# Sample attention with two score buffers, the second half's selection laid between the first half's products; 1 KB page pieces; a store issued later

## The reference

```python
kc, vc = compress(gather(cmp pages) ++ new)        # windows of 32 tokens, stride 16 -> two small products with a GELU
p_cmp = softmax(q @ kc + bias);    o_cmp = p_cmp @ vc
imp   = sum over a head group of p_cmp @ overlap   # importance of each block of 64 tokens
sel   = the blocks kept: 16 of 17, some always kept
p_sel = softmax(q @ k_sel + bias, only kept blocks); o_sel = p_sel @ v_sel   # the "sel" pages
p_win = softmax(q @ k_win + bias);  o_win = p_win @ v_win                    # the last 512 tokens
out   = g0 * o_cmp + g1 * o_sel + g2 * o_win
```

## Time and profile before

| | us |
|---|---|
| median of 3 runs | 1866.27 (1863.54 to 1869.59) |
| the profiled execution | 1865.92 |
| its span, first to last instruction | 1863.8 |
| `mixer_inputs` | 249.7 |
| `compress_phase` | 76.5 |
| `sample_attention` | 58.4 |
| the rest | 1479.2 |

### The profile page before, as it was taken

How to read it: one execution, slowest core, us unless ns; L and a number is a source line. 1 busy time by engine, 2 the same in 40 slices (tenths; PEclk the granted TensorE clock), 3 DMA queues, 4 the chain that set the end, 5 groups by cost and what they waited for, 6 DMA issues and landing times. The chain is left out here.

```text
span 1863.8 us, 28616 instructions
## 1 busy us (share of the span) xinstructions
PE 1775.2 (95%) x12010; PEld 1625.7 (87%) x12010; DVE 938.5 (50%) x1876; ACT 544.7 (29%) x1098; POOL 249.8 (13%) x110
## 2 busy tenths in 40 slices
PE   8999989589999899999978999999999999999997
PEld 6889978357767769999848999999999999999996
DVE  6422130467787664341533455545545555554547
ACT  7421000168888622210432221111111111111221
POOL 0111200000000000000000023313313322322320
PEclk9999999779999999999989999999999999999998
DMA  5122657621102241110261111101101101101102
GB/s 197 38 72 58 211 140 198 194 92 58 57 24 72 92 155 60 35 57 29 108 248 46 46 51 69 57 12 68 57 12 68 61 8 68 69 2 67 57 17 94
DMA packets 98308, 145.60 MB, mean 78 GB/s; under 512 B 40637, under 2 KB 73597, under 8 KB 96541
## 3 DMA queue, kind: packets, MB, share of 16 engines
q1 hardware_dynamic: 94094, 140.62, 22.7%
q10 hardware_dynamic: 4088, 3.17, 0.6%
HBM read 132.69 MB, written 14.19 MB: 79 GB/s over the span
## 5 line engine op out<-in xcount | busy, mean ns | idle before, releaser
L1963 PE MATMUL ps<-ff_in_high,ff_weights_low 128*128 128x352 f32 x1032 | 335.0, 325 | 0.0
L1963 PE MATMUL ps<-ff_in_high,ff_weights_high 128*128 128x352 f32 x1032 | 332.6, 322 | 0.0
L1963 PE MATMUL ps<-ff_in_low,ff_weights_high 128*128 128x352 f32 x1032 | 330.5, 320 | 0.0
L1963 PEld LDWEIGHTS ps<-ff_in_high,ff_weights_high 128*128 128x128 f32 x1032 | 194.4, 188 | 0.2
L1963 PEld LDWEIGHTS ps<-ff_in_low,ff_weights_high 128*128 128x128 f32 x1032 | 194.0, 188 | 0.2
L1963 PEld LDWEIGHTS ps<-ff_in_high,ff_weights_low 128*128 128x128 f32 x1032 | 193.7, 188 | 0.0
L2195 DVE TENSOR_TENSOR x<-ps,x 128x352 f32<-128x352 f32 x216 | 113.3, 524 | 134.6 <-PE ps L1981 134.6
L1932 POOL TENSOR_TENSOR ff_weights_low<-ff_weights,ff_weights_high 128x1024 fp32r<-128x1024 f32 x44 | 105.7, 2402 | 418.1 <-ACT ff_weights_high L2077 418.1
L1981 PE MATMUL ps<-ff_act_high,ff_down_high 128*128 128x352 f32 (+1 forms) x496 | 158.4, 319 | 0.2
L1981 PE MATMUL ps<-ff_act_high,ff_down_low 128*128 128x352 f32 (+1 forms) x496 | 156.6, 316 | 0.0
L1981 PE MATMUL ps<-ff_act_low,ff_down_high 128*128 128x352 f32 (+1 forms) x496 | 156.6, 316 | 0.0
(11 more groups left out here) (360 smaller groups left out, 3723.4 us busy)
## 6 DMA issues: line engine op xcount, KB each, us to landing
ff_weights<-in_w_up SPq DMA_DIRECT2D x22, 512.0 KB, 4.0
ff_weights<-in_w_gate SPq DMA_DIRECT2D x22, 512.0 KB, 4.3
ff_down<-in_w_down SPq DMA_DIRECT2D x22, 512.0 KB, 3.5
top<-in_mem_kt SPq DMA_DIRECT2D x8, 1024.0 KB, 10.9
top<-in_mem_v SPq DMA_DIRECT2D x8, 1024.0 KB, 13.5
x<-in_xt SPq DMA_DIRECT2D x3, 1408.0 KB, 10.0
x<-in_pool_cmp SPq DMA_DIRECT2D x32, 128.0 KB, 3.1
big<-in_pool_cmp SPq DMA_DIRECT2D x32, 128.0 KB, 2.8
```

What stands on the lines that cost most here:

```text
L1963: last = nc.tensor.matmul(K.bank[3 * s + x][:, 0:b - a], wt[:, s, ws], h[:, k, a:b], start=k + n == 0, stop=k == KD - 1 and n == 2)
```

## The change

Five edits go together.

1. A page lands as it lies in memory, keys and values side by side, 1 KB in one piece; `score`, `multiply` and `hidden_rows` read it with other strides.
2. At the start SP issues the first weight before the gains, and ACT runs one tiny instruction that needs no DMA, which brings its function table in.
3. The store `out_fm` moves from the end of `mixer_inputs` to `compress_phase`, behind the windows of half 0 and ahead of the sel pages of half 0.
4. In `compress_phase` round 0 waits for the first weight alone, round 1 for the second; the position sums of keys and values are made and closed one after the other, the second after round 0.
5. In `sample_attention` there are two places for scores and statistics. PE's order becomes: scores 0, importance 0, scores 1, transposes 0, then one importance step of half 1 and a third of half 0's products, three times, then the sums over the memory's squares, transposes 1, products 1. DVE adds half 1's bias before it copies half 0's transposed probabilities. ACT and DVE are reordered to fit.

```diff
--- before.py
+++ after.py
@@ -156,17 +156,13 @@
-    slots = K.slots[half]
-    if name == "cmp":
-        slots = slots.rearrange("p v (g t) -> p v g t", g=HKV)
     with sp.Fori(first, first + count) as n:
         sp.load(regs, K.page_table[0:1, bass.ds(n * NPAGE + half * (NS // 2) * NPAGE, NPAGE)])
         pages = [sp.snap(r, min_val=0, max_val=K.n_pool - 1) for r in regs]
         for b, page in enumerate(pages):
             of = K.pools[name][bass.ds(page, 1)]
-            of = of.rearrange("a p v g t -> (a p) v g t" if name == "cmp" else "a p v t -> (a p) v t")
-            to = slots[:, :, :, bass.ds(n * (NPAGE * PAGE // 2) + b * (PAGE // 2), PAGE // 2)] if name == "cmp" else \
-                slots[:, :, bass.ds(n * (NPAGE * PAGE) + b * PAGE, PAGE)]
+            of = of.rearrange("a p v g t -> (a p) (v g t)" if name == "cmp" else "a p v t -> (a p) (v t)")
+            to = K.slots[half][:, bass.ds(n * (NPAGE * 2 * PAGE) + b * (2 * PAGE), 2 * PAGE)]
             sp.dma_start(to, of).then_inc(K.slots_came[half], 16)
@@ -287,10 +283,11 @@
-            sp.dma_start(K.gains[:, :, :], I["gains"]).then_inc(const_came, 16)
             for kk in range(4):
                 a, b = GROUPS[0]
                 sp.dma_start(wv_landing[kk], I["w_v"][kk]).then_inc(wv_came[kk], 16)
+                if kk == 0:
+                    sp.dma_start(K.gains[:, :, :], I["gains"]).then_inc(const_came, 16)
                 sp.dma_start(K.XT[:, 2 * kk:2 * kk + 2, a:b], I["xt"][:, 2 * kk:2 * kk + 2, a:b]).then_inc(x_came[kk], 16)
@@ -340,9 +337,7 @@
                 sp.dma_start(O["win_old"][v], I["win_old"][v][:, TS:WIN, :]).then_inc(K.out_sem, 16)
             sp.wait_ge(done, 3 * CHUNKS)
             sp.dma_start(K.cmp_w1[1], I["w_cmp1"][1]).then_inc(K.cmp_w1_came[1], 16)
-            sp.wait_ge(taken, 3 * CHUNKS)
-            sp.dma_start(O["fm"].rearrange("c p n -> p c n"), K.FM[:, 4:8, :]).then_inc(K.out_sem, 16)
-            K.outs(6)
+            K.outs(5)
             sp.wait_ge(K.gates_sem, 16)
@@ -483,10 +478,13 @@
-            act.wait_ge(const_came, 16)
+            act.wait_ge(eps_set, 1)
+            nc.scalar.activation(K.stat[:, 0, 0:1], K.eps[:, :], ACT.Copy)
             for kk in range(4):
                 act.wait_ge(wv_came[kk], 16)
                 nc.scalar.activation(wv[:, 0, 2 * kk:2 * kk + 2, :], wv_landing[kk], ACT.Copy).then_inc(wv_high, 1)
+                if kk == 0:
+                    act.wait_ge(const_came, 16)
@@ -666,12 +664,12 @@
...
-    terms = ar[:, 16384:18432].rearrange("p (q h) -> p q h", h=P)
+    terms = [ar[:, o:o + 2048].rearrange("p (q h) -> p q h", h=P) for o in (16384, 8192)]
@@ -701,6 +699,8 @@
             gather(sp, K, 1, "cmp")
             sp.wait_ge(K.out_sem, 16 * K.outs(0))
             sample_windows(sp, K, I, 0)
+            sp.dma_start(O["fm"].rearrange("c p n -> p c n"), K.FM[:, 4:8, :]).then_inc(K.out_sem, 16)
+            K.outs(1)
             sp.wait_ge(first, 2)
...
             link(nc.vector.memset(ones, 1.0))
             for v in range(2):
                 dve.wait_ge(came_w[v], 16)
-                link(nc.vector.tensor_tensor(terms, w1[v], pe_t[v].unsqueeze(2).to_broadcast([P, 16, P]), ALU.mult))
-                link(nc.vector.tensor_reduce(sums[v], terms.rearrange("p q h -> p h q"), AX.X, ALU.add))
+                link(nc.vector.tensor_tensor(terms[v], w1[v], pe_t[v].unsqueeze(2).to_broadcast([P, 16, P]), ALU.mult))
+                link(nc.vector.tensor_reduce(sums[v], terms[v].rearrange("p q h -> p h q"), AX.X, ALU.add))
                 dve.sem_inc(summed, 1)
-            for v in range(2):
                 dve.wait_ge(pe_w1, v + 1)
                 nc.vector.tensor_tensor(hb[:, v:v + 1], K.bank[6 + v][:, v:v + 1], b1[:, v:v + 1], ALU.add).then_inc(biased, 1)
...
-            def bias():
-                for v in range(2):
-                    pe.wait_ge(summed, v + 1)
-                    nc.tensor.matmul(K.bank[6 + v][:, v:v + 1], sums[v], ones, start=True, stop=True).then_inc(pe_w1, 1)
+            def bias(v):
+                pe.wait_ge(summed, v + 1)
+                nc.tensor.matmul(K.bank[6 + v][:, v:v + 1], sums[v], ones, start=True, stop=True).then_inc(pe_w1, 1)
...
-            for v in range(2):
-                pe.wait_ge(came_w[v], 16)
             for n in range(len(rounds)):
+                if n < 2:
+                    pe.wait_ge(came_w[n], 16)
                 hidden_rows(n)
-                if n == 0:
-                    bias()
+                if n < 2:
+                    bias(n)
                 if n >= 1:
@@ -850,7 +848,8 @@
-    SC = ar[:, 12288:12288 + 1664]
+    tmp = K.top[:, O_TMP:O_TMP + 2 * D]
+    SCS = [ar[:, 12288:12288 + 1664], tmp[:, 0:1664]]
-    st = ar[:, a + 990:a + 1010]
+    sts, PCT = [ar[:, a + 990:a + 1010], tmp[:, 1792:1812]], tmp[:, 1664:1792]
-    mem_sq = K.top[:, O_TMP:O_TMP + KD * MEM].rearrange("p (c n) -> p c n", c=KD)
+    mem_sq = ar[:, 12288:12288 + KD * MEM].rearrange("p (c n) -> p c n", c=KD)
...
-            score(0)
-            for half in range(2):
-                VS, VW = K.slots[half][:, 1], K.windows[half][1]
-
-                pe.wait_ge(impu, 3 * half + 1)
-                nc.tensor.transpose(K.bank[4][:NCMP, 0:P], PC, K.ident[:, :]).then_inc(impt, 1)
-                pe.wait_ge(impu, 3 * half + 2)
-                nc.tensor.matmul(K.bank[4][:, 128:128 + NSEL], PT[:NCMP, 0, :], ovl[:NCMP, :], start=True, stop=True).then_inc(impt, 1)
-                pe.wait_ge(impu, 3 * half + 3)
-                nc.tensor.matmul(K.bank[4][:, 160:160 + NSEL], gm, imp, start=True, stop=True).then_inc(impt, 1)
-                if half:
-                    pe.wait_ge(mem_squared, 2)
-                    for c in range(KD):
-                        last = nc.tensor.matmul(K.bank[0][:, 0:MEM], K.ones[:, :], mem_sq[:, c, :], start=c == 0, stop=c == KD - 1)
-                    last.then_inc(mem_total, 1)
+            def importance(half, step):
+                bank = K.bank[4 if half == 0 else 0]
+                pe.wait_ge(impu, 3 * half + step + 1)
+                if step == 0:
+                    last = nc.tensor.transpose(bank[:NCMP, 0:P], PC, K.ident[:, :])
+                elif step == 1:
+                    last = nc.tensor.matmul(bank[:, 128:128 + NSEL], PCT[:NCMP, :], ovl[:NCMP, :], start=True, stop=True)
+                else:
+                    last = nc.tensor.matmul(bank[:, 160:160 + NSEL], gm, imp, start=True, stop=True)
+                last.then_inc(impt, 1)
...
+            def turn(half):
                 pe.wait_ge(pready, half + 1)
                 if half:
                     pe.wait_ge(otaken, half)
                 for i, (x, w) in enumerate(blocks):
                     b = i // 4
-                    last = nc.tensor.transpose(K.bank[4 + b][:w, (i % 4) * P:(i % 4 + 1) * P], SC[:, x:x + w], K.ident[:, :])
+                    last = nc.tensor.transpose(K.bank[4 + b][:w, (i % 4) * P:(i % 4 + 1) * P], SCS[half][:, x:x + w], K.ident[:, :])
                 last.then_inc(turned, 1)
-                if not half:
-                    score(1)
+
+            def multiply(half, first, end):
+                VS, VW = K.slots[half].rearrange("p (b v t) -> p b v t", v=2, t=PAGE)[:, :, 1], K.windows[half][1]
                 pe.wait_ge(ptaken, 2 * (half + 1))
-                for i, (x, w) in enumerate(blocks):
+                for i in range(first, end):
...
-                last.then_inc(pv, 1)
+                if end == 15:
+                    last.then_inc(pv, 1)
+
+            score(0)
+            for step in range(3):
+                importance(0, step)
+            score(1)
+            turn(0)
+            for step in range(3):
+                importance(1, step)
+                multiply(0, 5 * step, 5 * step + 5)
+            pe.wait_ge(mem_squared, 2)
+            for c in range(KD):
+                last = nc.tensor.matmul(K.bank[1][:, 0:MEM], K.ones[:, :], mem_sq[:, c, :], start=c == 0, stop=c == KD - 1)
+            last.then_inc(mem_total, 1)
+            turn(1)
+            multiply(1, 0, 15)
...
-            for half in range(2):
+            def add_bias(half):
+                SC, st = SCS[half], sts[half]
                 dve.wait_ge(scores, half + 1)
-                if half:
-                    dve.wait_ge(turned, half)
...
+            add_bias(0)
+            compressed(0)
+            selected(0)
+            weigh(0)
+            add_bias(1)
+            take(0)
+            compressed(1)
+            selected(1)
+            outputs(0)
+            weigh(1)
+            take(1)
             outputs(1)
...
+            exp(0, 0, c_cmp, c_end)
+            exp(0, 1, c_new + 32, c_cmp)
+            exp(0, 2, 0, c_new + 32)
+            exp(1, 0, c_cmp, c_end)
+            take(0)
+            exp(1, 1, c_new + 32, c_cmp)
+            act.wait_ge(mem_came, 16)
+            for h in range(2):
```

(52 more changed lines are left out.)

27 lines of the change are left out of this document (12 added, 15 removed).

## The result

The changed kernel takes 1851.41 us (median of 5, 1850.07 to 1855.0) against 1866.27: 0.9926 of it, 95% interval 0.991 to 0.9942. The forecast was 1865.8, with a range of 1858 to 1871.5. The profiled execution is the one of 1851.41, its span 1849.6.

The account below looks back on a forecast made before the run. PE, busy 95% of the span, and SP's queue feeding it were taken as the bound; start −1.3, barrier −0.4, compression −1.8 and sample attention +3.0 gave −0.5, median 1865.8 us, 8-in-10 range 1858 to 1871.5.

Parts of the forecast that it names:

- page layout: Page issue on SP: one piece per partition takes 566 ns like four or two, so the edit changes nothing.
- Rival A: Pages on SP's queue issue faster in one piece, 0.43 us for 0.566, saving 4.35 per 32; kernel 1856.0; chance 0.14.
- Compression, SP's side: Copies −2.0, store +0.8; SP's chain becomes the last at the barrier; the compression stage changes by −1.8 us.
- half 1's scores at the stage's start + 32: Sample attention: half 1's scores stay at start + 32.06 us, by SP's 28.80 of page issue and the landing.
- The copies' −2.0: Compression: SP's eight copies, 8.15 us, get 2.0 us shorter without the store among the transfers.
- The store's 0.8: Compression: the store moved ahead of the sel pages costs SP's chain 0.8 us, between 0.40 and 5.4.
- The start's −1.3: Kernel start: early table load and earlier weight let ACT start at the input's landing, 5.7 for 7.08; −1.3 us taken.
- The barrier's −0.4: First barrier, at 249.7: the store's issue no longer stands last on SP; −0.4 us, bounds 0 to −0.6.
- Sample attention: The stage grows by 3.0 us: +0.8 for DVE's copies, +1.3 and +0.9 for products between importance steps.
- The first third: 20 products of half 0 between importance 1 and 2: +1.3 us at half clock; the second third, before importance 3, +0.9.
- The rule on bursts: Trainium skill, PE's clock: product bursts shorter than the waits between them start cold; alone it puts all three thirds at half clock.
- rival B: Sample attention: half 1's chain falls to the low clock, transposes 3.46 for 1.80, stage +8.6 us; kernel 1871.4; chance 0.14.

Follow-up runs that it names:

- layout_undone: The changed kernel with edit 1 undone (pages land in four and two pieces again), all else as changed: 1869.38 us, 1.0014 to 1.0035 of before.
- probe: The changed kernel, also refetching cmp pages in seven forms while SP waits at the projections' end; only issue times read: half and quarter pages 345 ns.

## Why the prediction was wrong

**The step that failed is the page layout.** From the earlier trace rows, where four pieces and two cost the same 566 ns, it took that "one piece takes 566 too, and the edit costs and brings nothing". Both points were of rows that are cut; a row that is not cut is of another kind and issues in 342. Rival A had the right event at a chance of 0.14. Its price, 0.43, came from pieces of the input with fixed addresses, whose rows are cut in two as well (line 294), and was no lower bound: the same trace had loads at 341, so 0.34 could have been seen beforehand.

```profile
L288 SPq DMA_DIRECT2D x<-in_w_fm x6: 341/355/434, 52.8 to 135.8; - x6
```

**Two further terms hung on it.** One is *Compression, SP's side*: that PE waits for pages before round 4 and SP is the last at the barrier holds only with slow pages, in `layout_undone` (a wait of 7.5 before round 4, 0.2 of SP at the barrier). With 7.2 us a loop less, PE's chain ends last and gives its 7.2 (measured 7.4), as A said. The other is half 1's scores at the stage's start + 32, which came at 25.1. Of the 13.7 us between the forecast and the measured spans, 5.6 lie in the compression and 6.8 in the sample attention. The copies' −2.0 was right (8.15 to 5.55, −2.6). The store's 0.8 was too little: 2.37, and 1.8 of the longest page issue behind it. Both are off the path.

**The start's −1.3 was wrong.** It took the shortest landing time of four pieces, 4.1, for that of the first; in the changed kernel no piece landed in less than 5.3, and the first was waited for until 7.0. The 7.08 it started from is also not ACT's first useful instruction but the first that reads the input; the weight's copy stands ahead of it, and the table's load was already hidden behind the input's landing. The barrier's −0.4 came out at −0.6, the end of its bounds.

**Sample attention was right in kind and nearly in size, apart from the pages.** Half 1 waits for pages, not for the place; its chain is longer by 3.2 (forecast 3.0). But the sum fits better than its terms. The chain to the first importance product grew by 9.47 − 8.58 = 0.9 (forecast 0.8). Only 0.6 of that is behind the start of DVE's bias, where the copies stand (352.17 − 347.79 in place of 366.84 − 363.05); the other 0.3 lies in the scores.

```profile
347.79 0.22 DVE L997 TENSOR_TENSOR top<-ps,big 128x63 f32<-128x63 f32 x1 [9.11 <-PE ps L909]
```

The first third cost nothing (1.48 in place of 1.49, forecast +1.3) and the second 2.3 (forecast 0.9), since the lower clock came one third later than I put it: 0.53 from 354.20 on. That these two misses nearly cancel is luck. The rule on bursts that the prediction quotes speaks of waits between them; between these thirds PE had none, and the first of them, right behind a wait of 2.67, was the one at full clock (1.30 for the 40 records of its row; the last third took 2.52 for 40). Of rival B the third importance product came about (+2.1 to 2.2 there, 2.3 measured), but half 1's transposes took 1.80, so the rest of B did not.

## What to carry to other kernels

Where one engine only issues DMAs and another waits for them, look at the issue time of one DMA and at its form: two forms with the same price say little of a third of another kind. Before a stage is given more places or another order, find what its late half waits for last; a place that ends no wait brings nothing, and its new order can still cost. And when one chain gets shorter, price every other edit again: the same wait edit that would have been swallowed by slow pages was worth 6.7 us with fast ones.

## What was not expected of the hardware

By the medians of these runs, a page's DMA with its address in a register costs SP 342 to 348 ns when each partition gets one piece, of 256, 512 or 1024 bytes, and 564 to 612 when it gets two or four, on 32 partitions as on 128. And a store may hold the loads behind it in SP's queue for long: in `probe`, where two stores of 2 MB each from memory to memory were issued some 12 us before the pages of half 1, one page's issue took 6.5 us (0.54 at most in the changed kernel). No run isolates the cause:

```profile
L166 SPq DMA_DIRECT2D big<-in_pool_cmp x32: 337/343/6462, 258.7 to 290.9; - x32
```
